# Matmuls that nothing reads, at nine places of the mixers of a two-block language model kernel

## The reference, cut to what matters

```python
p = (u @ w_in).astype(jnp.float32)
p_pool, p_hg, p_rw, p_gla = jnp.split(p, [G, 5 * G, 5 * G + RWKV_COLS], axis=-1)
y_pool = causal_multiscale_pool(p_pool, pool_w, pool_b, pool_scale)
...
o_h = chunked_gated_linear_attention(split_heads(jax.nn.silu(hq) * QK_SCALE),
                                     split_heads(1.0 - f),
                                     split_heads(hi), split_heads(log_f)).reshape(B, T, G)
...
o_r = rwkv7_scan(r_h, split_heads(decay), k_h, v_h, kk, split_heads(a))
...
log_a = jax.nn.log_sigmoid(ga @ gla_w2 + gla_b) / GLA_GATE_TAU
o_g = chunked_gated_linear_attention(split_heads(gq * QK_SCALE), split_heads(gk),
                                     split_heads(gv), split_heads(log_a))
...
y = jnp.concatenate([y_pool, y_hgrn, y_rwkv, y_gla], axis=-1).astype(u.dtype)
return y @ w_out
```

## Time and profile before

| | us |
|---|---|
| median of three runs | 1919.37 |
| lowest, highest | 1915.62, 1919.42 |
| the profiled execution | 1914.36 |
| its span, first to last instruction | 1912.5 |
| PE busy | 1785.8 (93%) |
| DVE busy | 906.4 (47%) |
| ACT busy | 670.1 (35%) |
| mean granted clock of TensorE | 0.950 |

### The profile page before, as it was taken

The page is one execution under the profiler, slowest core; times in us unless marked ns, Lnnn a source line. Parts: engine busy times, 40 slices in busy tenths (PEclk is TensorE's granted clock), DMA queues, the critical chain, the costliest instruction groups (busy, mean ns, idle before and its releaser), DMA issues.

```text
span 1912.5 us, 22254 instructions
## 1 busy us (share of the span) xinstructions
PE 1785.8 (93%) x8686; PEld 1429.5 (75%) x8686; DVE 906.4 (47%) x1223; ACT 670.1 (35%) x1008; POOL 166.9 (9%) x145
## 2 busy tenths in 40 slices
PE   7999989998998799999999797988899899999997
PEld 5777767777776588888887676767887678888885
DVE  6524434532433554444335774667545544444322
ACT  5144654124553433332224324244122333233221
POOL 0001001001000100000004120120330100000000
PEclk9999999999998899999999897986899899999998
DMA  5302212322212122223333210110001123222331
GB/s 184 121 33 91 75 56 89 121 78 67 77 57 68 53 98 90 90 99 93 92 98 130 66 45 33 57 38 1 1 1 61 45 88 100 99 88 92 96 92 51
DMA packets 41240, 144.17 MB, mean 75 GB/s; under 512 B 4864, under 2 KB 4880, under 8 KB 40880
## 3 DMA queue, kind: packets, MB, share of 16 engines
q1 hardware_dynamic: 37152, 130.61, 21.0%
q0 software_dynamic: 2256, 9.00, 1.4%
q10 hardware_dynamic: 1728, 3.15, 0.5%
HBM read 140.63 MB, written 2.10 MB: 75 GB/s over the span
## 4 chain that ended last, share of the span: by engine, by line
PE 78%; DVE 12%; ACT 7%; issue 2%; DMA 0%; POOL 0%; DVEq 0%; ACTq 0%; POOLq 0%; SPq 0%
PE bank L414 22%; PE bank L415 21%; PE bank L416 21%; PE bank L396 8%; DVE sb_w_low L1016 2%; PE bank L402 2%; PE bank L583 1%; ACT sb_w_high L1689 1%; PE bank L562 1%; ACT L1689 1%; DVE sb_E L1016 1%; DVE sb_near L1356 1%; ACT sb_E L1689 1%; PE bank L519 1%; DVE sb_x L1024 1%
## 5 line engine op out<-in xcount | busy, mean ns | idle before, releaser
L1016 DVE TENSOR_TENSOR sb_w_low<-sb_raw,sb_w_high 128x1024 fp32r<-128x1024 f32 (+1 forms) x253 | 319.3, 1262 | 413.9 <-ACT sb_w_high L1689 410.1
L414 PE MATMUL bank<-sb_xg_high,sb_w_high 128*128 128x512 f32 x1176 | 477.6, 406 | 23.0 <-DVE sb_xg_low L1024 20.6
L415 PE MATMUL bank<-sb_xg_low,sb_w_high 128*128 128x512 f32 x1176 | 468.4, 398 | 0.0
L416 PE MATMUL bank<-sb_xg_high,sb_w_low 128*128 128x512 f32 x1176 | 468.2, 398 | 0.0
L1689 ACT ACTIVATE sb_w_high<-sb_raw 128x1024 fp32r<-128x1024 f32 (+1 forms) x253 | 263.2, 1040 | 397.5 <-PE bank L416 376.0
L414 PEld LDWEIGHTS bank<-sb_xg_high,sb_w_high 128*128 128x128 f32 x1176 | 224.2, 191 | 97.3 <-issue 32.5
L416 PEld LDWEIGHTS bank<-sb_xg_high,sb_w_low 128*128 128x128 f32 x1176 | 224.1, 191 | 52.8
L415 PEld LDWEIGHTS bank<-sb_xg_low,sb_w_high 128*128 128x128 f32 x1176 | 224.5, 191 | 52.0 <-issue 1.8
L414 PE MATMUL bank<-sb_h_high,sb_w_high 128*128 128x512 f32 x352 | 138.9, 395 | 0.0
L416 PE MATMUL bank<-sb_h_high,sb_w_low 128*128 128x512 f32 x352 | 138.9, 395 | 0.0
L415 PE MATMUL bank<-sb_h_low,sb_w_high 128*128 128x512 f32 x352 | 138.9, 395 | 0.0
(11 more groups left out here) (312 smaller groups left out, 2208.2 us busy)
## 6 DMA issues: line engine op xcount, KB each, us to landing
sb_raw<-w_ffn_in SPq DMA_DIRECT2D x88, 512.0 KB, 3.2
sb_raw<-w_ffn_out SPq DMA_DIRECT2D x32, 512.0 KB, 3.5
sb_raw<-w_tok SPq DMA_DIRECT2D x24, 512.0 KB, 3.3
sb_raw<-w_mix_f SPq DMA_DIRECT2D x18, 512.0 KB, 3.2
sb_raw<-w_rot SPq DMA_DIRECT2D x16, 512.0 KB, 3.5
sb_raw<-w_qk SPq DMA_DIRECT2D x16, 512.0 KB, 3.3
sb_raw<-w_out SPq DMA_DIRECT2D x16, 512.0 KB, 3.2
sb_raw<-w_ffn_out SPq DMA_DIRECT2D x16, 384.0 KB, 3.1
```

Of the source, the lines that this page charges most:

```text
L414: e.matmul(out, w[0], v[0], start=first, stop=False)
L415: e.matmul(out, w[0], v[1], start=False, stop=False)
L416: return e.matmul(out, w[1], v[0], start=False, stop=last)
L1016: e.tensor_tensor(out, a, b, op).then_inc(*v.up(*signal))
```

## The change

A new function takes a bank of the ring and multiplies `ones` by `inv_rms` into it, n times, as plain float32 of 128x512. Nobody reads the bank; its entry `freed_by` is None, so the bank's next taker does not wait. It is called at nine places, with 34 matmuls in all: before hgrn's `near` (4), before hgrn's `scores(0)` (4), after the projection `gla a` (7), after hgrn's last scores (3), in `operand_steps` before `sigma` (4), before gla's last scores (4) and after them (3), and before the first and the second `product` of the inverse (3 and 2).

```diff
+    def keep_busy(n):
+
+        i = take(("unread", turn[0]), None)
+        for _ in range(n):
+            e.matmul(banks[i][:, :], mem.ones, mem.inv_rms, start=True, stop=True)
+
     def mixers():
...
             fill(0)
+            if name == "hgrn":
+                keep_busy(4)
             for h in HEADS:
                 r, g = head_tile(h)
                 i = take(("near", name, h), ("near", name, h))
...
                 if n + 1 < len(ORDER):
                     fill(n + 1)
+                if n == (0 if name == "hgrn" else len(ORDER) - 1):
+                    keep_busy(4)
                 scores(n)
+            keep_busy(3)
             fill(len(ORDER))
...
             projected("gla a", 0, "gla a landed")
+            keep_busy(7)
             for f in range(2):
                 i = take(("gla gate", f), ("gla sized", f))
...
         def operand_steps():
             yield
+            keep_busy(4)
             for f in range(2):
...
+            if size == 2:
+                keep_busy(3)
             product(0)
+            if size == 2:
+                keep_busy(2)
             product(1)
```

## The result

Five executions of the changed kernel took 1921.72 to 1927.38 us, median 1925.88; five of the kernel before, on the same chip, 1915.05 to 1919.42, median 1915.66. The estimated ratio is 1.0041, 95% interval [1.0023, 1.0058]; the ratio of the two medians, 1.0053, lies inside it. The change makes the kernel slower by about 0.4%, twice what the prediction took such a measurement to tell from no change. The time lies in the predicted range, near its upper end; "within 0.2%", the likeliest sign of the forecast, did not come. The profiled execution took 1926.38 us, 12.0 more than that of before.

A forecast was written before the change was run, and what follows sets the result against it. The prediction took TensorE, busy for 93% of the span, to bound the kernel. Its terms 1.5 + 0 + 1.7 + 0 - 1.2 + 0.9 gave +2.9 us on an average of 1917.2: 1920.1 us, range 1912 to 1927.

The forecast's parts named there:

- within 0.2%: Sign for the whole kernel: the time differs from the kernel before by at most 0.2%, 3.8 us; chance 0.46.
- Part 1: Before hgrn's near and scores(0): the first four matmuls start at half clock after the y_pool wait; +1.5 us, high end +2.9.
- Part 2: After gla a: seven matmuls fit the 9.6 us wait for DVE, 0; if the clock survives, first gate 0.9 us sooner.
- Part 3: After hgrn's last scores: three matmuls start when the wait ends and delay gla's values; +1.7 us, from -0.4 to +2.3.
- Part 4: In operand_steps: four matmuls lie in the wait for ACT's tanh; 0.
- Part 5: Around gla's last scores: mixed runs at full clock but bonus waits for rE; -1.2 us, far end +2.3 through late exponentials.
- Part 6: Inverse: the shorter ring makes head 1's X step wait for DVE's mask, delaying product(3); +0.9 us, far end +2.4.
- slower rival: New matmuls in hgrn run at half clock in the path and the ring of six adds waits; +6.4 us, 1923.6, chance 0.27.
- faster rival: Fillers hold the clock at the gates, before gla's values, into bonus and the transposes; -5.9 us, 1911.3, chance 0.22.

The follow-up runs named there:

- j_all_dense: The whole change, with the inverse's five matmuls and two takes replaced by ten matmuls in banks due next; 1914.57 us, ratio 1.0002 to the kernel before.
- h: The kernel before plus only the seven matmuls around gla's last scores; 1921.15 us, ratio 1.0040.
- k: The kernel before plus seven matmuls around gla's last scores, six before bonus and ten in the inverse; 1911.07 us, ratio 0.9979.
- m: k without its one matmul before product(3); 1910.39 us, ratio 0.9976 to the kernel before.
- o: m plus the change's four matmuls before hgrn's scores(0) and seven after gla a; 1911.57 us, ratio 0.9976 to the kernel before.
- d_same_bank: The kernel before plus the inverse's five matmuls, written to the bank the next product takes anyway; 1923.86 us, ratio 1.0040.
- l_hgrn_parts: The kernel before plus ten matmuls in the inverse, and the change's matmuls before near, before scores(0) and after hgrn's last scores; 1919.10 us, ratio 1.0016.
- c_two_takes: The kernel before plus the two takes of a bank at the inverse, with no matmul in them; 1925.94 us, ratio 1.0062.
- a_no_inverse: The change without its five matmuls and two takes at the inverse; 1926.43 us, ratio 1.0056 to the kernel before.
- n_after_scores: m with no matmuls before gla's last scores and four after them; 1907.62 us, ratio 0.9951 to the kernel before.
- the third set: Four follow-up runs, l_hgrn_parts, m, n_after_scores and o, sharing their runs of the kernel before, which measured 1915.38 us.
- the second: Set of four follow-up runs, h, j_all_dense, k and one with only ten matmuls in the inverse; the kernel before measured 1915.12 us.

## Why the prediction was right and where it was wrong

The range held, and the sum's direction was right; the size was not: +2.9 us forecast, +10.2 by the medians, +7.9 by the estimated ratio. Of the rivals the slower one, 1923.6, came nearest. That the range held is luck in part. 5.5 of the 7.0 us between the sum and its high end were the far ends of parts 1, 3 and 5, which did not come and made room for part 6; and the range was laid on 1917.2, while the kernel before measured 1915.66 beside the change. Part by part, by shifts in the profiled execution:

- **Part 1, +1.5.** Right in every step. The new matmuls start at the end of the `y_pool` wait at half clock and take 5.89 us; near takes 2.8, and DVE takes its results 4.0 late; scores(1) is at full clock. DVE regained 2.1 of its forecast 2.5 us. Measured +2.1.
- **Part 2, 0 (or -0.9).** The clock held in this execution: the gates' four instructions take 1.95 us, DVE's shift drops from 1.86 to 0.92. In j_all_dense, the same code here, they take 3.75. The uncertain case was priced rightly, and is one of chance.
- **Part 3, +1.7.** The three take 5.10 us, the values start at 1173.11 against the forecast 1172.8; +1.3 on DVE, of which 0.7 is gone by 1228.
- **Part 4, 0.** No shift arises between 1228 and `rE`.
- **Part 5, -1.2.** Right to about a tenth (-1.3 measured): mixed takes 9.0 us instead of 17.1, TensorE then idles 6.38 us for `rE`, bonus and the transposes stay at half, and the shift goes from +1.5 to +0.2. Its far end, late exponentials (+3.5), did not show here, where the four before scores(8) took 3.70 us; where they took 5.2 to 5.4 (h, j, k, m, o) it was 0.2 to 0.4.
- **Part 6, +0.9, far end +2.4: the step that failed.** The mechanism was seen in part: the ring, the mask, the fall in the short waits, the two steps at half clock. They put product(3) 2.5 us late, the far end. What the step did not ask is how long the clock stays down after such a fall. I priced half clock for the two steps ahead of product(3) and took the 70.84 us behind it as given, at full clock, because the row says so. They contain about 19 us that can be at half, worth 8 to 9 us. The measured term is +11.4, and d_same_bank shows the part behind product(3) by itself: 10.5 with product(3) on time.

The Trainium skill's rule weighed there ("TensorE: Matmul & The Clock Gate", "A second HAM failure mode: psum-queue depth-cycling") has the clock swing with brief idling between groups. The trace agrees that it fell, with waits of 1.2 to 1.9 us around it, but the +2.4 worked out beside it was still a fifth of the loss.

The slower rival named the half clock of places 1 and 3 and the ring as its mechanism. Places 1 and 3 did what parts 1 and 3 said and no more (l_hgrn_parts), and the ring is sufficient (c_two_takes) but not necessary (d_same_bank, a_no_inverse). With the ring gone or the fillers gone the loss was the same, so what the rival, the part and my first theory all lacked was the stretch behind product(3). The faster rival failed where forecast, in the idle time before bonus; with work put there it is real, as n_after_scores shows.

**Open.** What precisely decides whether the clock returns at 1354 was not isolated. Without any change the kernel before seems to lose it now and then: one of its 29 executions beside the third set took 1925.93 us at a mean clock of 0.943, and one of the 27 beside the second took 1922.84 at 0.944, against 0.950 for most. No trace of those executions was taken.

## What to carry to other kernels

Before adding anything ahead of a long stretch in which TensorE alone sets the time, look at when the clock comes back before that stretch; if it is back only a microsecond or two earlier, any delay, wait or shorter ring ahead of it can stake the whole stretch. Where filler, matmuls that nothing reads, is used to hold the clock, it should reach up to that stretch and, close to it, write to a bank that is due anyway, since two takes alone cost 0.62% here. Filler that covers only the first waits moves the fall from where it is free to where it is paid. Even so nothing is certain: with a last wait of 2.01 us left, the clock held in the traces of m and n and fell in that of o, and with that wait partly filled it fell for 3.4 us in that of k. And a part that measures as a loss alone can be a gain once the clock is held in the critical stretch: place 5 alone cost 0.40%, and with bonus and the inverse filled it belongs to a version 0.21% faster.

## What the runs showed of the hardware that was not expected

- A TensorE that never idles need not get its clock back soon. In the changed kernel it is busy 4.00 of 4 us in every stretch from 1356 on, with the products and steps of the inverse, and the clock stays at 0.50 until about 1378; in a_no_inverse it is so from 1352 until about 1380. After the waits in hgrn, before, it was back 4.3 to 4.6 us after the restart, and it is back within the 5.89 us that the first new matmuls take after the `y_pool` wait: near, behind them, takes 2.82 us.
- A new matmul, two instructions, costs 0.90 us at full clock by the rows of four (3.60 us), and 0.86 from the first start to that of what follows; the prediction took 0.98 from the key norm.
